# Four elementwise products of a chunked RWKV-7 scan, moved from between the levels of an inverse to a place ahead of them

## The reference

```
def wkv7_scan(S0, r, decay, k, v, kk, a):
    # S_t = S_{t-1} (diag(w_t) - kk_t^T (a_t * kk_t)) + v_t^T k_t ;  y_t = S_t r_t
    def step(S, inp):
        r_t, w_t, k_t, v_t, kk_t, a_t = inp
        sa = jnp.einsum('bhvk,bhk->bhv', S, -kk_t)
        S = (S * w_t[:, :, None, :] + sa[..., None] * (kk_t * a_t)[:, :, None, :]
             + v_t[..., None] * k_t[:, :, None, :])
        return S, jnp.einsum('bhvk,bhk->bhv', S, r_t)
    ...
    S, y = lax.scan(step, S0, xs)
```

## Time and profile before

| | |
|---|---|
| median of 3 runs | 1992.53 us (1992.5 to 1997.03) |
| profiled execution | 1992.53 us, span 1990.8 us |
| mean granted TensorE clock | 0.951 of full speed |
| busy: TensorE, weight loads, VectorE, ScalarE, GpSimd | 1783.4, 1047.1, 627.2, 392.3, 365.0 us |
| scan of the prompt (L1201) | 326.5 to 453.6 us |
| sample group's steps on GpSimd | about 344 to 594 us |
| first expert weights issued | 760.7 us |

### The profile page before, as it was taken

The page is one execution under the profiler, slowest core; times in us unless marked ns, Lnnn a source line. Parts: engine busy times, 40 slices in busy tenths (PEclk is TensorE's granted clock), DMA queues, the critical chain, the costliest instruction groups (busy, mean ns, idle before and its releaser), DMA issues. The chain is left out here.

```text
span 1990.8 us, 29270 instructions
## 1 busy us (share of the span) xinstructions
PE 1783.4 (90%) x10614; PEld 1047.1 (53%) x10614; DVE 627.2 (32%) x1516; ACT 392.3 (20%) x918; POOL 365.0 (18%) x529
## 2 busy tenths in 40 slices
PE   8999997998999999999988888888888888888887
PEld 6857776887778885645433333333333333333332
DVE  1387754873214312611211111111111111111127
ACT  0114544552120101311111111111111111111112
POOL 1000000888871000011110101111111111111100
PEclk8999998999999999999998989998989898989998
DMA  4443312011233324479999999999999999999965
GB/s 120 147 141 102 97 46 49 3 35 36 79 119 109 119 76 190 198 283 420 421 420 410 419 405 410 419 414 398 411 408 396 411 410 396 413 410 417 409 284 241
DMA packets 160782, 532.04 MB, mean 267 GB/s; under 512 B 22061, under 2 KB 88927, under 8 KB 110205
## 3 DMA queue, kind: packets, MB, share of 16 engines
q1 hardware_dynamic: 138921, 488.47, 62.3%
q0 software_dynamic: 20640, 41.23, 5.5%
q10 hardware_dynamic: 1148, 1.34, 0.2%
HBM read 522.52 MB, written 41.42 MB: 283 GB/s over the span
## 5 line engine op out<-in xcount | busy, mean ns | idle before, releaser
L1944 PE MATMUL bank<-arena 128*64 128x512 f32 x2048 | 513.6, 659 | 139.0 <-DMA arena<-in_w_e 137.8
L1944 PEld LDWEIGHTS bank<-arena 128*64 128x64 f32 x2048 | 159.0, 151 | 489.1 <-issue 487.7
L1962 PE MATMUL bank<-arena 128*64 128x512 f32 x1024 | 233.8, 598 | 0.0
L2187 DVE TENSOR_TENSOR arena<-bank,arena 128x256 f32<-128x256 f32 x64 | 27.2, 425 | 579.1 <-ACT arena L2032 579.1
L1812 POOL DMA_INDIRECT arena<-h_rows,index x66 | 67.1, 1016 | 772.1 <-DVE index L2061 714.2
L1431 PE MATMUL bank<-arena 128*128 128x276 f32 x768 | 184.7, 399 | 7.3 <-ACT arena L1533 3.1
L1431 PEld LDWEIGHTS bank<-arena 128*128 128x128 f32 x768 | 146.5, 191 | 41.6 <-ACT arena L1533 3.5
L2032 ACT ACTIVATE arena<-bank 128x256 f32<-128x256 f32 x64 | 24.7, 386 | 604.5 <-PE bank L1944 604.5
L1201 PE MATMUL bank<-arena 64*64 64x64 f32 (+2 forms) x2816 | 119.6, 239 | 16.4 <-DVE arena L1300 8.7
L1962 PEld LDWEIGHTS bank<-arena 128*64 128x64 f32 x1024 | 67.8, 136 | 110.9 <-issue 109.7
L1201 PEld LDWEIGHTS bank<-arena 64*64 64x64 f32 x2816 | 105.0, 135 | 22.7 <-DVE arena L1300 9.0
(11 more groups left out here) (333 smaller groups left out, 1842.3 us busy)
## 6 DMA issues: line engine op xcount, KB each, us to landing
arena<-in_w_e SPq DMA_DIRECT2D x384, 1024.0 KB, 14.2
arena<-in_w_in SPq DMA_DIRECT2D x50, 512.0 KB, 4.2
arena<-routed_rows SPq DMA_DIRECT2D x8, 2048.0 KB, 23.0
arena<-in_w_mem_kv SPq DMA_DIRECT2D x4, 1024.0 KB, 5.7
arena<-in_cache_mem_k SPq DMA_DIRECT2D x8, 512.0 KB, 4.8
arena<-in_cache_mem_v SPq DMA_DIRECT2D x8, 512.0 KB, 5.5
arena<-in_w_out SPq DMA_DIRECT2D x2, 2048.0 KB, 12.6
arena<-in_w_s SPq DMA_DIRECT2D x3, 1024.0 KB, 10.7
```

The lines of the kernel that those rows point to most:

```text
L1944: mm = pe.matmul(p_gu[t * S:(t + 1) * S, :], xt[:, v, c, t * S:(t + 1) * S], w13[2 * v + t][:, :, c, :], start=(c == 0), stop=(c == KD - 1))
L1962: mm = pe.matmul(p_y[h][t * S:(t + 1) * S, :], hidT[:, j, t * S:(t + 1) * S], w2[2 * v + t][:, j, h * 512:(h + 1) * 512], start=(j == 0), ...
```

## The change

`vectors` loses its argument x and issues its four products in one go. In `chunk`, the call for chunk n + 1 stands behind the masking of the four tiles and ahead of level 1, where it was one product behind each of levels 1 to 4. The products themselves, their order, their operands and the semaphore they raise stay as they are. The other engines' programs don't change.

```
-        def vectors(n, u, x):
-
+        def vectors(n, u):
             cols = ds(n * CH, CH)
-            if x == 0:
-                dve.tensor_tensor(qri[u][:, :, 0, :], kkey[:, :, cols], before[:, :, cols], ALU.mult)
-            elif x == 1:
-                dve.tensor_tensor(bvec[u], bkey[:, :, cols], up[:, :, cols], ALU.mult)
-            elif x == 2:
-                dve.tensor_tensor(qri[u][:, :, 1, :], rec[:, :, cols], down[:, :, cols], ALU.mult)
-            else:
-                dve.tensor_tensor(kvec[u], key[:, :, cols], up[:, :, cols], ALU.mult).then_inc(s_bd, 1)
+            dve.tensor_tensor(qri[u][:, :, 0, :], kkey[:, :, cols], before[:, :, cols], ALU.mult)
+            dve.tensor_tensor(bvec[u], bkey[:, :, cols], up[:, :, cols], ALU.mult)
+            dve.tensor_tensor(qri[u][:, :, 1, :], rec[:, :, cols], down[:, :, cols], ALU.mult)
+            dve.tensor_tensor(kvec[u], key[:, :, cols], up[:, :, cols], ALU.mult).then_inc(s_bd, 1)
...
                 dve.tensor_tensor(ys[:, p], b(p)[:, 0:256].rearrange("p (q t) -> p q t", q=4), masks[:, 1:5], ALU.mult)\
                    .then_inc(s_mb, 1)
+            if more:
+                vectors(n + 1, 1 - u)
             for lv in range(1, LEVELS):
...
-                if more and lv < LEVELS - 1:
-                    vectors(n + 1, 1 - u, lv - 1)
...
-        for x in range(4):
-            vectors(0, 0, x)
+        vectors(0, 0)
```

## The result

The changed kernel takes 2010.33 us in the median of 6 runs (2005.78 to 2011.72), beside 1992.47 us of the kernel before in the same session: 1.0086, 95% interval 1.0067 to 1.0103. That is 17.9 us more, where I forecast 10.5. A second series of the same kernel gave 2008.06 us beside 1992.10, 1.0081 (1.0065 to 1.0098). Slower as forecast and inside the range, by about 1.6 times the size; both medians lie where the rival of the clock has them (2008 to 2010 us), above the 2000 to 2008 us to which I gave 0.66.

The account below looks back on a forecast made before the run. TensorE was taken to lead the scan, VectorE close behind. Delay of 18.3 us to growth 1, less 4.2 cover, less 4.6 removed, gave +9.5, taken as +10.5 on 1992.5: 2003.0 us, range 1994 to 2012.

Parts of the forecast that it names:

- the rival of the clock: In the scan, new level-2 stalls make TensorE's clock fall in three or four chunks: +5 to +7 us, 2008 to 2010; chance 0.15.
- What bounds, and whether it passes through: TensorE leads the scan, VectorE close behind; a late scan moves merge and expert loads, nothing absorbing it within 1 to 2 us.
- Turns with GpSimd: In chunks 1 to 6, products alternate with GpSimd instructions, one each; a turn costs GpSimd's step of about 1.23 us.
- the strict price: VectorE and GpSimd fully block each other: 1.52 us a turn, at most 5.2 us more over six chunks.
- The walk: Block lengths from each chunk's start in GpSimd's 14.75 us cycle; with chunk 0's 1.4, 18.8 us in all.
- Stalls at level 2: TensorE waits for the late level-1 growths: 18.3 us of delay less 4.2 of cover, 14.1 us.
- Cover: VectorE's free time before growth 1 (0.35 us) plus slack behind it (0.25): 0.60 us a chunk, 4.2 over seven.
- What is removed: TensorE's 13 weight-load waits on L1317, at levels 3 and 5 of the scan, go wholly: gain 4.6 us.
- that the block holds GpSimd off: Each block costs 1.4 to 1.6 us without turns, or meets mostly pauses and sums: +0.6 to +3 us; chance 0.15.
- That the products fit into free time: Stalls at levels 3 and 5 go and none comes at level 2: 1987.9 us, faster; chance 0.04.

Follow-up runs that it names:

- the control: The changed kernel run once more, unaltered, beside the run with wide idle TensorE matmuls: 2008.06 us, scan 142.1 us.
- Without the steps: The changed kernel with the arithmetic of the sample group's steps on GpSimd left out: 1991.36 us (0.9991), scan 122.7 us.
- the kernel before without the steps: The kernel before with the arithmetic of the sample group's steps on GpSimd left out: 1987.99 us (0.9974), scan 119.2 us.
- the chunk of 20.68 us above: From the changed kernel without GpSimd's sample-step arithmetic, plus four idle VectorE products of 128x512 behind each block: 2018.66 us, scan 152.9 us.
- the first filling: The changed kernel with 24 short idle TensorE matmuls a chunk ahead of the level-2 wait in chunks 1 to 6: 2009.17 us (1.0072).

## Why the forecast was right, and where it was short

**What bounds, and whether it passes through:** right. The merge's matmuls start 21.0 us later, where I had 9 to 12; 17.4 us of it are the scan's. The first expert load comes 20.8 us later with a scan 17.4 longer and a start 3.6 later, and in the control 18.5 later with 15.0 and 3.7.

**Turns with GpSimd:** right, with the price per turn that the rows gave. In chunk 5 four products start GpSimd's step of 1.10 to 1.23 us apart. Only 10 of the 24 products in chunks 1 to 6 are that long, though; the others meet the short row sums or a pause and take 0.41 to 0.94 us. The means by line are 0.60 to 0.95 us, where I had said "near 1 us". The Trainium skill (SBUF — State Buffer, "Who interferes with whom") has it that whoever issues first keeps the other out for the whole instruction. The trace agrees for a product that meets a GpSimd instruction: it waits for the end. It doesn't agree the other way round: GpSimd's L1164 starts at 428.09, 0.13 us ahead of the end of L1292, and isn't longer for it. So the strict price, an estimate of 1.52 us a turn, is not what a turn of 256 elements costs here.

**The walk:** its sum was near and its chunks were wrong. I had 2.1, 4.1, 4.2, 1.9, 1.6 and 3.5 us for chunks 1 to 6, 17.4 in all; measured 3.93, 2.26, 2.35, 3.10, 4.82 and 2.34, 18.8 in all, and 3.93, 2.26, 2.35, 3.09, 3.18 and 3.09 in the control, 17.9. In the first profile each chunk is off by 1.2 to 3.2 us, three up and three down, so that the sum came out is in part luck. The start of the walk can't be read from one trace: GpSimd's first L1155 starts 20.2 us behind the scan in the kernel before, and 17.3 and 15.7 us behind it in the two profiles of the changed one. The blocks of chunk 1 thus start 6.7 and 7.9 us into GpSimd's cycle, where I had 2.9. From there the two launches run in step, with blocks 11.6, 13.6 and 1.4 us into it in chunks 2, 3 and 4 of both; why they come together isn't shown. The fall in chunk 4 parts them again, and chunk 5 meets all of the long run in one launch (4.82 us) and not in the other (3.18).

**Stalls at level 2:** 14.1 us forecast; 15.7 measured, and 14.1 in the control.

**Cover:** 0.60 us a chunk forecast, and about that measured. The seven blocks make 20.3 us in all, less 7 x 0.08 = 19.7, against stalls of 15.7: a cover of 4.0 us, 0.58 a chunk. In the control it is 18.8 - 14.1 = 4.7, 0.67 a chunk. Without the steps it is larger, 1.34 - 0.47 = 0.87 us, since in the kernel before without the steps VectorE idles 0.54 us ahead of growth 1 in every chunk, and with them 0.35 in the mean.

**What is removed:** all waits at levels 3 and 5 went, as forecast, but 4.6 us was too much for their worth. The matmuls saw only 2.4 us of them. This term was 2.2 us too large.

**The clock:** this is the term that was mis-sized most. I had it at zero in the sum and as a rival with 0.15, which asked for three or four falls and 5 to 7 us. Measured: 13.6 us at 1.2 GHz in the first profile, falls of 3.4, 3.4 and 6.8 us, and two falls of 3.4 in the control. At 1.5 to 1.6 us for 3.4 and 2.5 for 6.8 (the chunk of 20.68 us above) that is some 5.6 and 3.1 us. The whole can be added up from what TensorE does. Over the scan it is busy for 126.8 us and not 119.6 (+7.2), its matmuls wait 12.3 us more on growths (14.7 - 2.4) and 1.7 less on masks: 17.8, where the scan is 17.4 longer. In the control +4.1 busy (123.7), +10.7 on growths (13.1) and +0.5 on masks (5.4) make 15.3 of 15.0. The falls are most of the busy time added; 1.0 to 1.6 us of it beyond their price stay open. What misled me was the row of 487 to 491 us in the earlier trace rows, a pause of 2.4 us without a fall, from which I took it that only the longest blocks matter. But the control has its two falls behind stalls of 2.2 and 2.4 us and none behind those of 3.2 and 2.7. At this length falls are a matter of chance from launch to launch (last section), and seven new stalls are seven tickets.

**The rivals:** that the block holds GpSimd off is refuted by chunk 5 of the changed kernel. That the products fit into free time is refuted by the 15.7 us. The rival of the clock was no rival but a part: turns and falls together give the time, and neither alone does.

## What to carry to other kernels

Work that is "free" on VectorE is priced by what GpSimd does at that moment: with both inputs in SBUF beside long GpSimd instructions on SBUF (1.04 to 1.09 us here), each VectorE product took a GpSimd step of 1.10 to 1.23 us, so a row of four can cost four steps, while one in each gap costs only what the gap doesn't cover. Price a TensorE wait by its matmuls, not by its weight loads. Before moving work, read which engine is behind it on the queue and how much of a turn the slack there covers. And price a new TensorE stall with its clock: add the expected falls behind it, not only its length.

## What the runs showed of the hardware

A pause of TensorE of the same length may or may not be followed by half clock. In the front of this kernel TensorE pauses for 2.4 us at 300 to 303 us and again at 307 to 312 us, in all fourteen profiled launches. In five of them (the changed kernel twice, the kernel before the second time, the first filling, the four products behind growth 5) half clock for 3.4 us follows each of the two, and the scan starts at 329.8 to 330.4 us; in the nine others it doesn't, and it starts at 324.1 to 326.5. Between the pauses lie 7.3 us without the fall and 8.8 to 9.0 with it, and behind the second 8.0 and 9.7 us up to the next pause. The two falls so cost 3.3 us before the changed code runs, a good part of the spread of the kernel before (1987.1 to 1998.6 us in 21 runs). Windows of the front of the kernel before, in its second profile (the pauses lie at 303.1 and 312.0 us, the falls behind them):

```profile
303.00:305.30 2.30, 0.07 (x1) 0.00 (x0) 1.29 (x4) 2.11 (x3) 0.00 (x0) 1.00 0.00 0
305.30:308.70 3.40, 3.24 (x7) 2.52 (x8) 0.71 (x2) 2.39 (x2) 0.00 (x0) 0.50 0.02 5
308.70:312.00 3.30, 3.25 (x14) 2.28 (x12) 0.00 (x0) 0.01 (x1) 0.00 (x0) 1.00 0.00 0
312.00:315.50 3.50, 1.16 (x5) 1.02 (x6) 2.00 (x4) 2.91 (x4) 0.00 (x0) 1.00 0.00 0
315.50:318.90 3.40, 3.40 (x14) 2.75 (x13) 1.59 (x4) 0.41 (x4) 0.00 (x0) 0.51 0.00 0
```

Inside the scan the falls are 3.4 or 6.8 us long. Behind the pause of 8.7 us just ahead of the scan there is one in all fourteen launches, of 10.2 us. A fall of 3.4 us costs 1.5 to 1.7 us where TensorE has matmuls to do.
